# Feed-forward blocks with the tokens as stationary operand, gate and up in one 512-column product, the hidden product turned on TensorE, and the norm's root applied as a scale

## The chip, the cores and the metric

The kernel runs on one core of a Trainium2 chip. TensorE (PE) multiplies, VectorE (DVE) and ScalarE (ACT) do the elementwise work, GpSimd (POOL) a little of it, and the queue of SyncE (SP) issues the loads of the weights. The metric is the device time of one execution in microseconds (us); lower is better. Matrices are float32, at most 128 partitions high.

## The reference

The program is two layers of one block and one layer of a second block on 256 tokens of width 1024. Five feed-forwards of hidden width 2816 lie in it: two in each of the first two layers, one in the last. The change is about them and about nothing else.

```python
def rms_norm(x, gain):
    xf = x.astype(jnp.float32)
    y = xf * lax.rsqrt(jnp.mean(xf * xf, axis=-1, keepdims=True) + EPS)
    return (y * gain.astype(jnp.float32)).astype(x.dtype)

def swiglu_ffn(h, w_in, w_out):
    gate, up = jnp.split(h @ w_in, 2, axis=-1)
    return (jax.nn.silu(gate) * up) @ w_out

    for l in range(DEPTH):
        x = x + FFN_RESID * swiglu_ffn(rms_norm(x, ffn1_norm[l]), ffn1_w_in[l], ffn1_w_out[l])
...
        x = x + FFN_RESID * swiglu_ffn(rms_norm(x, ffn2_norm[l]), ffn2_w_in[l], ffn2_w_out[l])
...
        h = h + _swiglu(_rmsnorm(h, norm_ffn_g[l]), w_gate[l], w_up[l], w_down[l])
```

The root of the norm is one number per token. It can be taken out of a product: with g the gain and r the root's reciprocal, (x * r * g) @ w is r times (x * g) @ w.

## The kernel before

**Numbers in two halves.** A product of two float32 matrices is made of three products of a faster 32-bit form (`fp32r`): each operand is split into a rounded part `hi` and the rest `lo`, and TensorE adds hi by hi, hi by lo and lo by hi (`three`, L237 to 241). ACT makes `hi` by a copy (`split_act`, L453), DVE makes `lo` by a subtraction (`split_vec`, L459), for the weights as for the activations.

**Tokens.** The 256 tokens lie in two tiles of 128 (`m`). `x` holds them with tokens on the partitions. For a product they must lie with the width on the partitions: TensorE turns 128x128 squares into one of four banks `turn` (`norm_pe`, L367 to 375), DVE multiplies by the gain on the way to `xT` (L343), then ACT and DVE make `xT_hi` and `xT_lo` (L387, L392). `quarter b` is one half of the width of one tile.

**The feed-forward.** The hidden width is cut into 11 blocks of 256. A block takes two chunks of weights of 1 MB, one of gate and one of up, through a ring of four slots that SP fills (`ffn_sync`). In `block` (L465) the weights are the stationary operand, 128 columns at a time, and all 256 tokens move past them: four groups of 8 steps of three matmuls, 96 matmuls with 256 columns. Gate lands in one bank of `acc`, up in the other, hidden width on the partitions. ACT takes the silu of the gate bank (L554), DVE multiplies by the up bank (L584), and the product is already turned as the second product needs it: ACT copies `hT_hi` (L559), DVE makes `hT_lo` (L590). The split weights `w_hi` and `w_lo` have room for two blocks, so the split of block j+1 begins when block j-1 is done. After the 11 blocks, `down` (L506) multiplies by 11 chunks of `w_out`; there the tokens are the stationary operand and 512 columns of weights move. Its last four chunks are used for tile 0 first, so that tile 0 is ready four half steps before tile 1.

**The opening of a feed-forward** is the place between two products. DVE adds the product to `x` (L612), ACT takes the sum of squares (L310) and the root (L313), DVE its reciprocal (L337) and the scaled `xn` (L339), TensorE turns it, and the chain above follows. To have work in that time, TensorE does the first gate chunk without a split, in plain float32 and tile by tile (`first_gate`, L494); DVE and ACT split the first up chunk meanwhile.

**What sets the order.** Each engine runs a list written out by hand (`ffn_pe`, `ffn_act`, `ffn_vec`, `norm_act`, `add_norm_vec`), in order, and waits on counting semaphores. Nothing is scheduled by a tool: an instruction that waits holds back all behind it on its engine. `between` is the place in the last product of a stage at which TensorE turns tile 0 for the next one; `asides` are parameters of the next stage.

The openings are of three kinds: at the **start** of the program; after an output projection (**projection to feed-forward**, three times: both layers and the last); and from the second feed-forward of layer 0 straight into the first of layer 1 (**feed-forward to feed-forward**, once).

## Time and profile before

| | us |
|---|---|
| Median of 3 runs | 1775.39 (1773.43 to 1776.05) |
| The profiled execution | 1776.37 |
| Its span in the trace | 1774.7 |
| PE busy (share of the span) | 1747.2 (98%) |
| DVE busy | 1037.3 (58%) |
| ACT busy | 826.7 (47%) |

The profiled execution lies 0.98 us above the median of the runs, and 1.7 us of it lie outside the span. The granted TensorE clock was 0.997 of full speed on average. TensorE's matmuls overlap in the records (the next starts while the last drains), so the distance from start to start is what one costs.

### The profile page before, as it was taken

Reading aid. Unit: us, or ns where it says so; the run is one execution under the profiler, and the core shown is the slowest. Engines: PE = TensorE matmul, PEld = TensorE weight load, DVE = VectorE, ACT = ScalarE, POOL = GpSimd, SP = SyncE. Lnnn points to the kernel's source line nnn. Section 1 sums busy time; section 2 is a strip of 40 time slices with the busy share of each in tenths; the row PEclk is TensorE's granted clock in tenths of the full one; section 3 lists DMA queues with packets and bytes.
Section 4 is the critical chain, followed back from the end, with each engine's and each line's share of the span. In section 5 each row is a group of like instructions: output and inputs, shape, how many; then the busy total and the mean of one; then the engine's idle time right before and its main releaser. Section 6 shows DMA issues by size and latency. Waiting matters only on the chain.

```text
span 1774.7 us, 27727 instructions
## 1 busy us (share of the span) xinstructions
PE 1747.2 (98%) x11748; PEld 1545.3 (87%) x11748; DVE 1037.3 (58%) x1224; ACT 826.7 (47%) x913; POOL 71.0 (4%) x121
## 2 busy tenths in 40 slices
PE   8999999999999999999999999999999899999998
PEld 8998797887999899987978889998888766889996
DVE  5455466977655455454668785446688525644553
ACT  5544355563654445553555645455233114445442
POOL 0000000000000000000000000200191000000000
PEclk9999999999999999999999999999999999999999
DMA  7547254544655645372554446846347224356371
GB/s 261 189 137 281 83 182 156 159 149 143 221 176 185 225 153 179 120 281 89 186 164 144 145 143 233 161 160 236 121 158 138 65 80 144 118 170 205 100 286 58
DMA packets 202510, 292.13 MB, mean 165 GB/s; under 512 B 16834, under 2 KB 137908, under 8 KB 202420
## 3 DMA queue, kind: packets, MB, share of 16 engines
q1 hardware_dynamic: 201492, 290.21, 49.4%
q0 software_dynamic: 608, 0.60, 1.1%
q8 instruction: 70, 1.15, 0.3%
q14 instruction: 20, 0.16, 0.0%
q10 hardware_dynamic: 320, 0.01, 0.0%
HBM read 288.96 MB, written 1.84 MB: 164 GB/s over the span
## 4 chain that ended last, share of the span: by engine, by line
PE 92%; DVE 5%; DMA 2%; issue 1%; ACT 1%; ACTq 0%; DVEq 0%; SPq 0%
PE acc L239 24%; PE acc L240 23%; PE acc L241 23%; PE acc L286 3%; PE acc L2808 2%; DMA ring<-in_ffn_w_in 2%; PE acc L222 2%; PE acc L3118 1%; PE acc L494 1%; PE acc L207 1%; PE turn L2870 1%; PE acc L268 1%; PE turn L374 1%; PE acc L1353 1%; PE turn L1458 1%
## 5 line engine op out<-in xcount | busy, mean ns | idle before, releaser
L461 DVE TENSOR_TENSOR w_lo<-ring,w_hi 128x2048 fp32r<-128x2048 f32 x160 | 361.8, 2290 | 208.6 <-ACT w_hi L457 208.5
L239 PE MATMUL acc<-xT_hi,w_hi 128*128 128x256 f32 x1680 | 476.8, 284 | 2.9 <-DVE w_lo L461 2.1
L240 PE MATMUL acc<-xT_lo,w_hi 128*128 128x256 f32 x1680 | 476.2, 283 | 0.0
L241 PE MATMUL acc<-xT_hi,w_lo 128*128 128x256 f32 x1680 | 476.1, 283 | 0.0
L457 ACT ACTIVATE w_hi<-ring 128x2048 fp32r<-128x2048 f32 x160 | 300.8, 1911 | 142.9 <-PE acc L241 99.6
L239 PEld LDWEIGHTS acc<-xT_hi,w_hi 128*128 128x128 f32 x1680 | 322.6, 192 | 4.1 <-DVE w_lo L461 2.3
L241 PEld LDWEIGHTS acc<-xT_hi,w_lo 128*128 128x128 f32 x1680 | 322.7, 192 | 0.0
L240 PEld LDWEIGHTS acc<-xT_lo,w_hi 128*128 128x128 f32 x1680 | 322.6, 192 | 0.0
L239 PE MATMUL acc<-w_hi,hT_hi 128*128 128x512 f32 x440 | 172.6, 392 | 0.0
L241 PE MATMUL acc<-w_hi,hT_lo 128*128 128x512 f32 x440 | 171.3, 389 | 0.0
L240 PE MATMUL acc<-w_lo,hT_hi 128*128 128x512 f32 x440 | 171.3, 389 | 0.0
L554 ACT ACTIVATE big<-acc 128x512 f32<-128x512 f32 x55 | 32.9, 597 | 229.4 <-PE acc L241 229.4
L584 DVE TENSOR_TENSOR big<-big,acc 128x512 f32<-128x512 f32 x55 | 37.8, 687 | 152.9 <-ACT big L554 152.9
L240 PE MATMUL acc<-ring_lo,normed_hi 128*128 128x512 f32 (+2 forms) x288 | 108.4, 376 | 0.0
L239 PEld LDWEIGHTS acc<-w_hi,hT_hi 128*128 128x128 f32 x440 | 82.6, 188 | 18.9 <-ACT big L554 2.1
L241 PEld LDWEIGHTS acc<-w_hi,hT_lo 128*128 128x128 f32 x440 | 82.6, 188 | 17.2
L240 PEld LDWEIGHTS acc<-w_lo,hT_hi 128*128 128x128 f32 x440 | 82.7, 188 | 16.6
L310 ACT ACTIVATE xn<-x 128x1024 f32<-128x1024 f32 x20 | 21.2, 1058 | 130.2 <-DVE x L612 129.8
L235 DVE TENSOR_TENSOR ring_lo<-ring,part_hi 128x2048 fp32r<-128x2048 f32 x28 | 63.3, 2286 | 9.0 <-ACT part_hi L230 9.0
L612 DVE SCALAR_TENSOR_TENSOR x<-acc,x 128x512 f32<-128x512 f32 x36 | 24.0, 688 | 71.0 <-PE acc L241 71.0
L240 PEld LDWEIGHTS acc<-ring_lo,normed_hi 128*128 128x128 f32 x288 | 54.1, 188 | 9.3
L230 ACT ACTIVATE part_hi<-ring 128x2048 fp32r<-128x2048 f32 x28 | 52.8, 1915 | 14.7 <-DMA ring<-in_w_out 10.8
(543 smaller groups left out, 2878.5 us busy)
## 6 DMA issues: line engine op xcount, KB each, us to landing
ring<-in_ffn_w_in SPq DMA_DIRECT2D x88, 1024.0 KB, 6.0
ring<-in_w_in SPq DMA_DIRECT2D x52, 1024.0 KB, 5.1
ring<-in_ffn_w_out SPq DMA_DIRECT2D x44, 1024.0 KB, 6.2
ring<-in_w_branch SPq DMA_DIRECT2D x12, 1024.0 KB, 5.0
ring<-in_w_out SPq DMA_DIRECT2D x12, 1024.0 KB, 5.0
ring<-in_w_gate SPq DMA_DIRECT2D x11, 1024.0 KB, 5.1
ring<-in_w_up SPq DMA_DIRECT2D x11, 1024.0 KB, 6.3
ring<-in_w_down SPq DMA_DIRECT2D x11, 1024.0 KB, 5.4
```

What stands on the lines that cost most here:

```text
L222: ins = pe.matmul(acc[bank(G, m)][:, :], aT[:, 4 * i + k, m * P:(m + 1) * P], slot(c + i, 4, 512)[:, k, :], start=(i == 0 and k == 0), sto ...
L230: act.activation(hi[:, e % RING], slot(c, k, n), ACT.Copy).then_inc(s.hi, 1)
L235: vec.tensor_tensor(slot_lo(c, k, n), slot(c, k, n), hi[:, e % RING].bitcast(F32), ALU.subtract).then_inc(s.lo, 1)
L239: pe.matmul(o, a_hi, wh, start=start, stop=False)
L240: pe.matmul(o, a_hi, wl, start=False, stop=False)
L241: return pe.matmul(o, a_lo, wh, start=False, stop=stop)
L286: ins = pe.matmul(acc[bank(G, q)][:, (f % 2) * TOK:(f % 2) * TOK + TOK], w[:, k % kc, f * P:(f + 1) * P], aT[:, k, :], start=(k == 0), sto ...
L457: act.activation(w_part(w_hi, r), raw_part(c0, r), ACT.Copy).then_inc(f.hi, 1)
L461: vec.tensor_tensor(w_part(w_lo, r), raw_part(c0, r), w_part(w_hi, r).bitcast(F32), ALU.subtract).then_inc(f.lo, 1)
L554: act.activation(gate_s[:, jj % 2], acc[bank(G0 + jj, 0)][:, :].rearrange("p (k n) -> p k n", k=2), ACT.Silu).then_inc(acc_read[bank(G0 + ...
L584: vec.tensor_tensor(h_s[:, jj % 2], gate_s[:, jj % 2], acc[bank(G0 + jj, 1)][:, :].rearrange("p (k n) -> p k n", k=2), ALU.mult).then_inc( ...
L2808: ins = pe.matmul(acc[bank(G, m)][:, :], memT[:, 4 * i + k, m * P:(m + 1) * P], slot(c, 4, 512)[:, k, :], start=(i == 0 and k == 0), stop= ...
```

## The change

In all five feed-forwards:

- The tokens become the stationary operand. The two chunks of a block stand side by side as one moving operand of 512 columns, gate in 0 to 255 and up in 256 to 511. A block is 2 tiles by 8 steps by three matmuls, 48 matmuls with 512 columns, each tile in a bank of its own.
- The hidden product then has tokens on its partitions. TensorE turns it (`turn_hidden`), 4 squares of 128x128 for a block, between the two tiles of the next block; the last block's turn lies in the first step of `down`. `hT_hi` and `hT_lo` are made from the bank `turn`.
- The norm is folded (`Fold`, `fold_act`, `fold_vec`, `fold_turn_pe`): TensorE turns `x` itself; the root's reciprocal enters as the scale of the silu and as the scalar of DVE's multiplication (one `scalar_tensor_tensor`). `xn` is no longer made there, and nothing of the product waits for the root.
- The first gate chunk is split like all others and multiplied in `fp32r`. At the start of the program, where chunks land one after another, the first block is done in two halves of 256 columns.
- The release of split room goes by whole blocks (`r | 1`). For the third and fifth feed-forward the two halves of the split room are swapped (`swap`), so that the first chunks can be split while the last product still runs.
- The last four chunks of `down` are used for tile 1 in the order 8, 9, 7, 10 (before: 7, 8, 9, 10), and in the second feed-forward `between` comes one step earlier.

The norms ahead of the mixers, the mixers, the cross attention and the final norm are as before.

```diff
-            def first_gate():
-                if not turned:
-                    norm_pe(pe, n, tiles=(0,))
-                wait_chunk(pe, c0)
-                wait_acc_free(pe, G0, 0)
-                for m in range(MT):
-                    if m == 1:
-                        norm_pe(pe, n, tiles=(1,))
-                    for ft in range(2):
...
+            def first_block():
+                wh, wl = w_pair(f, w_hi, 0), w_pair(f, w_lo, 0)
+                for c, width, chunks in ((0, FB, 1), (FB, FB, 2)) if n.first else ((0, 2 * FB, 2),):
+                    cs = slice(c, c + width)
+                    for m in range(MT):
+                        o, ms = acc[bank(G0, m)][:, cs], slice(m * P, (m + 1) * P)
+                        if m == 0:
+                            pe.wait_ge(f.hi, f.w0 + chunks)
+                        if c == 0:
+                            pe.wait_ge(n.act, n.hi(2 * m + 1))
+                            wait_acc_free(pe, G0, m)
                         for k in range(KD):
-                            if ft == 0 and k % 4 == 0:
-                                pe.wait_ge(n.vec, n.turned(2 * m + k // 4))
-                            ins = pe.matmul(acc[bank(G0, 0)][:, ft * TOK + m * P:ft * TOK + (m + 1) * P],
-                                            raw_part(c0, 0)[:, k, ft * P:(ft + 1) * P], xT[:, k, m * P:(m + 1) * P],
-                                            start=(k == 0), stop=(k == KD - 1))
-                ins.then_inc(products_done, 1)
-            first_gate()
-            pe.wait_ge(n.vec, n.v0 + SPLIT_DONE)
-            block(0, halves=(1,))
-            block(1)
-            with pe.Fori(1, PAIRS) as i:
-                block(0, i)
+                            pe.matmul(o, xT_hi[:, k, ms], wh[:, k, cs], start=(k == 0), stop=False)
+                        if c == 0:
+                            pe.wait_ge(n.vec, n.lo(2 * m + 1))
+                        for k in range(KD):
+                            if c == 0 and m == 0 and k == 4:
+                                fold_turn_pe(pe, n, 1)
+                            pe.matmul(o, xT_lo[:, k, ms], wh[:, k, cs], start=False, stop=False)
+                        if m == 0:
+                            pe.wait_ge(f.lo, f.w0 + RING + chunks)
+                        for k in range(KD):
+                            ins = pe.matmul(o, xT_hi[:, k, ms], wl[:, k, cs], start=False, stop=(k == KD - 1))
+                        if chunks == 2 and m == 0:
+                            ins.then_inc(f.tile, 1)
+                ins.then_inc(products_done, 2)
...
+            def turn_hidden(jj, i=0):
+                for m in range(MT):
+                    wait_acc_read(pe, G0 + jj, m, i)
+                pe.wait_ge(f.hT_lo, f.h0 + jj + 1 + 2 * i)
+                for ft in range(2):
+                    for m in range(MT):
+                        ins = pe.transpose(turn[2 + jj % 2][:, ft * TOK + m * P:ft * TOK + (m + 1) * P],
+                                           h_s[:, jj % 2, m, ft * P:(ft + 1) * P], ident[:, :])
+                ins.then_inc(f.turned, 1)
+            def block(jj, i=0):
+                pe.wait_ge(f.lo, f.w0 + RING + 2 * jj + 2 + RING * i)
+                products(jj, 0, i).then_inc(f.tile, 1)
+                turn_hidden(jj - 1, i)
+                products(jj, 1, i).then_inc(products_done, 2)
...
+        def fold_act(act, n, f, c0):
+            def root(m):
+                n.there(act, m)
+                act.activation(xn[:, m, :], x[:, m, :], ACT.Square, accum_out=stat[:, m:m + 1]).then_inc(n.act, 1)
+                act.wait_ge(n.act, n.rooted(m) - 1)
+                act.activation(stat[:, 2 + m:3 + m], stat[:, m:m + 1], ACT.Sqrt, bias=eps_col[:, 0:1],
+                               scale=1.0 / D).then_inc(n.act, 1)
+            def halves(m):
+                for b in range(2 * m, 2 * m + 2):
+                    act.wait_ge(n.vec, n.turned(b))
+                    act.activation(quarter(xT_hi, b), quarter(xT, b), ACT.Copy).then_inc(n.act, 1)
+            root_there_act(act)
+            if not n.first:
+                split_act(act, f, c0, 0)
+                split_act(act, f, c0, 1)
+            root(0)
+            halves(0)
+            split_act(act, f, c0, 0 if n.first else 2)
+            halves(1)
+            root(1)
+            if n.first:
+                split_act(act, f, c0, 1)
+                split_act(act, f, c0, 2)
+            split_act(act, f, c0, 3)
...
+        def fold_vec(vec, n, f, c0, gain, add=None, weights_first=False):
...
+            if add:
+                add(vec, 0, 0)
+                if weights_first:
+                    add(vec, 1, 0)
+                    split_vec(vec, f, c0, 0)
+                add(vec, 0, 1)
+                if weights_first:
+                    split_vec(vec, f, c0, 1)
+            turned(0)
+            turned(1)
+            rest(0)
+            rest(1)
+            scale(0)
+            if not weights_first:
+                split_vec(vec, f, c0, 0)
+            if add:
+                if not weights_first:
+                    add(vec, 1, 0)
+                add(vec, 1, 1)
+            if not weights_first and not n.first:
+                split_vec(vec, f, c0, 1)
+            turned(2)
+            turned(3)
+            rest(2)
+            rest(3)
+            if n.first:
+                split_vec(vec, f, c0, 1)
+                scale(1)
+                split_vec(vec, f, c0, 2)
+            else:
+                split_vec(vec, f, c0, 2)
+                scale(1)
+            split_vec(vec, f, c0, 3)
...
+            for j, i in enumerate((KF // 2 - 3, KF // 2 - 2, KF // 2 - 4, KF // 2 - 1)):
+                if between and j == (2 if f.q == 1 else 3):
                     between(pe)
...
-            def silu(jj, i=0):
-                wait_products(act, c0 + 2 * jj + 1, i)
-                act.activation(gate_s[:, jj % 2], acc[bank(G0 + jj, 0)][:, :].rearrange("p (k n) -> p k n", k=2),
-                               ACT.Silu).then_inc(acc_read[bank(G0 + jj, 0)], 1)
+        def ffn_act(act, f, n, c0, G0, asides={}):
+            def silu(jj, m, i=0):
+                if m == 0:
+                    act.wait_ge(f.tile, f.h0 + jj + 1 + 2 * i)
+                else:
+                    wait_products(act, c0 + 2 * jj + 1, i)
+                act.activation(gate_s[:, jj % 2, m, :], acc[bank(G0 + jj, m)][:, 0:FB], ACT.Silu,
+                               scale=stat[:, 4 + m:5 + m]).then_inc(f.gate, 1)
...
-            def hidden(jj, i=0):
-                wait_acc_read(vec, G0 + jj, 0, i)
-                vec.tensor_tensor(h_s[:, jj % 2], gate_s[:, jj % 2], acc[bank(G0 + jj, 1)][:, :].rearrange(
-                    "p (k n) -> p k n", k=2), ALU.mult).then_inc(acc_read[bank(G0 + jj, 1)], 1)
+            def hidden(jj, m, i=0):
+                vec.wait_ge(f.gate, 2 * f.h0 + 2 * jj + m + 1 + 4 * i)
+                vec.scalar_tensor_tensor(out=h_s[:, jj % 2, m, :], in0=acc[bank(G0 + jj, m)][:, FB:2 * FB], scalar=stat[:, 4 + m:5 + m],
+                                         in1=gate_s[:, jj % 2, m, :], op0=ALU.mult,
+                                         op1=ALU.mult).then_inc(acc_read[bank(G0 + jj, m)], 1)
```

In the lists below `chunk_landed` is the ring's semaphore, `x` at an `acc_read` wait means both adds of a tile, and `x2` counts equal instructions in a row.

DVE, the opening from a projection to a feed-forward (layer 0), before:

```order
L612 SCALAR_TENSOR_TENSOR x<-acc,x 128x512 [waits tile0_done] x2
L337 RECIPROCAL stat<-stat 128x1 [waits norm_act_steps]
L339 TENSOR_SCALAR xn<-x,stat 128x1024 [waits norm_vec_steps]
L612 SCALAR_TENSOR_TENSOR x<-acc,x 128x512 [waits products_done]
L343 TENSOR_TENSOR xT<-turn,col 128x4x128 [waits norm_pe_steps] x2
L612 SCALAR_TENSOR_TENSOR x<-acc,x 128x512 [waits products_done]
L392 TENSOR_TENSOR xT_lo<-xT,xT_hi 128x4x128 [waits norm_act_steps] x2
L337 RECIPROCAL stat<-stat 128x1 [waits norm_act_steps]
L339 TENSOR_SCALAR xn<-x,stat 128x1024 [waits norm_vec_steps]
L343 TENSOR_TENSOR xT<-turn,col 128x4x128 [waits norm_pe_steps] x2
L461 TENSOR_TENSOR w_lo<-ring,w_hi 128x8x256 [waits w_hi_ready]
L392 TENSOR_TENSOR xT_lo<-xT,xT_hi 128x4x128 [waits norm_act_steps] x2
```

and now:

```order
L748 SCALAR_TENSOR_TENSOR x<-acc,x 128x512 [waits tile0_done]
L748 SCALAR_TENSOR_TENSOR x<-acc,x 128x512 [waits products_done]
L492 TENSOR_TENSOR w_lo<-ring,w_hi 128x8x256 [waits w_hi_ready]
L748 SCALAR_TENSOR_TENSOR x<-acc,x 128x512 [waits tile0_done]
L492 TENSOR_TENSOR w_lo<-ring,w_hi 128x8x256 [waits w_hi_ready]
L532 TENSOR_TENSOR xT<-turn,col 128x4x128 [waits norm_pe_steps] x2
L538 TENSOR_TENSOR xT_lo<-xT,xT_hi 128x4x128 [waits norm_act_steps] x2
L543 RECIPROCAL stat<-stat 128x1 [waits norm_act_steps]
L748 SCALAR_TENSOR_TENSOR x<-acc,x 128x512 [waits products_done]
L532 TENSOR_TENSOR xT<-turn,col 128x4x128 [waits norm_pe_steps] x2
L538 TENSOR_TENSOR xT_lo<-xT,xT_hi 128x4x128 [waits norm_act_steps] x2
L492 TENSOR_TENSOR w_lo<-ring,w_hi 128x8x256 [waits w_hi_ready]
```

The first two splits of weights (L492) have moved ahead of the second add of tile 0 and ahead of the work on the turned tile.

ACT at the same opening, before:

```order
L298 ACT_TABLE_LOAD
L298 ACTIVATE stat<-eps_col 128x1
L310 ACTIVATE xn,stat<-x 128x1024 [waits acc_read2,acc_read0]
L313 ACTIVATE stat<-stat,eps_col 128x1 [waits norm_act_steps]
L457 ACTIVATE w_hi<-ring 128x8x256 [waits products_done,chunk_landed1]
L387 ACTIVATE xT_hi<-xT 128x4x128 [waits norm_vec_steps] x2
L310 ACTIVATE xn,stat<-x 128x1024 [waits acc_read3,acc_read1]
L313 ACTIVATE stat<-stat,eps_col 128x1 [waits norm_act_steps]
L387 ACTIVATE xT_hi<-xT 128x4x128 [waits norm_vec_steps] x2
```

and now:

```order
L324 ACT_TABLE_LOAD
L324 ACTIVATE stat<-eps_col 128x1
L488 ACTIVATE w_hi<-ring 128x8x256 [waits products_done,chunk_landed0]
L488 ACTIVATE w_hi<-ring 128x8x256 [waits products_done,chunk_landed1]
L506 ACTIVATE xn,stat<-x 128x1024 [waits acc_read2,acc_read0]
L508 ACTIVATE stat<-stat,eps_col 128x1 [waits norm_act_steps]
L514 ACTIVATE xT_hi<-xT 128x4x128 [waits norm_vec_steps] x2
L488 ACTIVATE w_hi<-ring 128x8x256 [waits products_done,chunk_landed2]
L514 ACTIVATE xT_hi<-xT 128x4x128 [waits norm_vec_steps] x2
L506 ACTIVATE xn,stat<-x 128x1024 [waits acc_read3,acc_read1]
L508 ACTIVATE stat<-stat,eps_col 128x1 [waits norm_act_steps]
L488 ACTIVATE w_hi<-ring 128x8x256 [waits products_done,chunk_landed3]
```

Both splits of the first two chunks (L488) stand ahead of the squares of tile 0, and no table is loaded between them and the last split.

PE, the first block at the same place, now (before it were 16 plain matmuls, a turn of tile 1, 16 more, and 48 of 256 columns):

```order
L267 MATMUL acc<-part_hi,xT_rest 128x512
L592 MATMUL acc<-w_hi,xT_hi 128x512 x8
L598 MATMUL acc<-w_hi,xT_lo 128x512 x4
L500 MATMUL turn<-ident,x 128x128 x8
L598 MATMUL acc<-w_hi,xT_lo 128x512 x4
L602 MATMUL acc<-w_lo,xT_hi 128x512 x8
L592 MATMUL acc<-w_hi,xT_hi 128x512 x8
L598 MATMUL acc<-w_hi,xT_lo 128x512 x8
```

The turn of tile 1 (L500) stands in the middle of tile 0's second group and is fed by `x`, no longer by `xn`.

## Rows read from the trace of the kernel before

**Rows 1.** The page, busy time and instructions of each engine.

```profile
PE 1747.2 (98%) x11748; PEld 1545.3 (87%) x11748; DVE 1037.3 (58%) x1224; ACT 826.7 (47%) x913; POOL 71.0 (4%) x121
```

**Rows 2.** Groups by line and form: busy us, mean ns | idle before, releaser.

```profile
L239 PE MATMUL acc<-xT_hi,w_hi 128*128 128x256 f32 x1680 | 476.8, 284 | 2.9 <-DVE w_lo L461 2.1 <-DVE xT_lo L392 0.8
...
L461 DVE TENSOR_TENSOR w_lo<-ring,w_hi 128x2048 fp32r<-128x2048 f32 x160 | 361.8, 2290 | 208.6 <-ACT w_hi L457 208.5
...
L457 ACT ACTIVATE w_hi<-ring 128x2048 fp32r<-128x2048 f32 x160 | 300.8, 1911 | 142.9 <-PE acc L241 99.6 <-DMA ring<-in_ffn_w_in 32.5 <-DMA ring<-in_ffn_w_out 5.0
...
L240 PEld LDWEIGHTS acc<-w_lo,hT_hi 128*128 128x128 f32 x440 | 82.7, 188 | 16.6
```

**Rows 3.** Timeline of PE in a steady gate and up block: start us, us, instruction.

```profile
60.04 0.28 PE L239 MATMUL acc<-xT_hi,w_hi 128*128 128x256 f32 x1
...
63.64 0.28 PE L239 MATMUL acc<-xT_hi,w_hi 128*128 128x256 f32 x1
```

**Rows 4.** Timeline of PE in the second product, 512 columns.

```profile
160.36 0.39 PE L239 MATMUL acc<-w_hi,hT_hi 128*128 128x512 f32 x1
...
162.40 0.39 PE L239 MATMUL acc<-w_hi,hT_hi 128*128 128x512 f32 x1
```

**Rows 5.** Timeline of PE, five squares turned between matmuls (layer parameters).

```profile
178.72 0.23 PE L998 MATMUL turn<-ident,vecs 77*128 77x77 f32 x1
178.79 0.60 PE L1000 MATMUL turn<-ident,ws_in 128*128 128x128 f32 x4
179.15 0.47 PE L239 MATMUL acc<-w_hi,hT_hi 128*128 128x512 f32 x1
179.46 0.39 PE L240 MATMUL acc<-w_lo,hT_hi 128*128 128x512 f32 x1
```

**Rows 6.** Timeline of PE, eight squares turned between matmuls (tile 0 of a norm).

```profile
635.83 1.03 PE L374 MATMUL turn<-ident,xn 128*128 128x128 f32 x8
...
636.62 0.47 PE L239 MATMUL acc<-w_hi,hT_hi 128*128 128x512 f32 x1
...
636.94 0.39 PE L240 MATMUL acc<-w_lo,hT_hi 128*128 128x512 f32 x1
```

**Rows 7.** Timeline of ACT, silu of the first block at the start.

```profile
25.32 0.60 ACT L554 ACTIVATE big<-acc 128x512 f32<-128x512 f32 x1 [2.50 <-PE acc L241]
```

**Rows 8.** Timeline, opening after a projection: first adds (DVE), first silu (ACT).

```profile
442.20 1.29 DVE L612 SCALAR_TENSOR_TENSOR x<-acc,x 128x512 f32<-128x512 f32 x2 [5.99 <-PE acc L241]
...
463.41 0.60 ACT L554 ACTIVATE big<-acc 128x512 f32<-128x512 f32 x1 [2.50 <-PE acc L241]
```

**Rows 9.** The same two rows of the opening between two feed-forwards.

```profile
627.87 1.29 DVE L612 SCALAR_TENSOR_TENSOR x<-acc,x 128x512 f32<-128x512 f32 x2 [6.57 <-PE acc L241]
...
654.47 0.60 ACT L554 ACTIVATE big<-acc 128x512 f32<-128x512 f32 x1 [2.50 <-PE acc L241]
```

**Rows 10.** Timeline at the start: PE's turn, ACT's copies and a root.

```profile
8.30 1.73 PE L374 MATMUL turn<-ident,xn 128*128 128x128 f32 x8
...
10.12 1.31 ACT L387 ACTIVATE xT_hi<-xT 128x512 fp32r<-128x512 f32 x2 [4.31 <-DVE xT L343]
11.34 1.04 ACT L310 ACTIVATE xn<-x 128x1024 f32<-128x1024 f32 x1
...
12.50 0.29 ACT L313 ACTIVATE stat<-stat,eps_col 128x1 f32<-128x1 f32 x1
```

**Rows 11.** Timeline of PE, two long waits in the last layer's mixer.

```profile
1379.19 2.46 PE L2745 MATMUL turn<-ident,big 128*128 128x128 f32 x16 [1.75 <-DVE big L2718]
...
1394.54 1.09 PE L2790 MATMUL turn<-ident,big 128*128 128x128 f32 x8 [3.56 <-DVE big L2783]
```

**Rows 12.** Stretches around these waits: busy us of engines, PEclk, DMA share, GB/s.

```profile
1375.00:1385.00 10.00, 7.54 (x124) 6.15 (x113) 9.56 (x19) 0.31 (x1) 0.00 (x0) 1.00 0.01 2
...
1395.00:1405.00 10.00, 9.89 (x96) 8.00 (x94) 2.50 (x7) 3.39 (x8) 0.00 (x0) 0.83 0.00 0
```

**Rows 13.** DMA view of 440 to 480 us, GB/s in each of 40 us.

```profile
GB/s 374 37 0 0 0 0 169 388 369 161 250 365 347 24 25 17 0 0 27 265 389 360 374 387 386 385 387 348 382 386 378 377 361 373 387 312 37 6 0 0
```

## What the change will do to the time

> **What bounds the kernel now.** The busy shares come first: TensorE works in 98% of the span [rows 1]. That says where the limit is, not how hard TensorE works, so the groups by line come second. In the gate and up products of one feed-forward, L239 to 241, TensorE runs three groups of 1680 matmuls, DVE's subtractions wait for ACT's copies and ACT's copies for TensorE [rows 2]; TensorE itself waited 2.9 us in 477 there. Third is the distance from start to start in the timeline, the price of one matmul. With 256 columns, 30 matmuls take 63.64 - 60.04 = 3.60 us, 0.1200 each [rows 3]; a block of 96 takes 11.52. With 512 columns and the tokens stationary, 9 take 2.04, 0.2267 each [rows 4]. So only what TensorE is given to do, and what it waits for at the openings, can change the time.
>
> **Steady blocks: the matmuls.** 48 matmuls of 512 columns replace 96 of 256: 48 x 0.2267 = 10.88 us against 11.52, a gain of 0.64 a block. The row for 512 columns has the same roles (tokens stationary, weights moving) and the same number form, so I take it as it is. Ten blocks of each of five feed-forwards are of this kind: 50 x 0.64 = 32.0 us gained.
>
> **Steady blocks: the turns.** Each block now has 4 squares turned. Where 5 squares stood between matmuls, one of them 77 wide, the first matmul should have started at 178.72 and the second at 178.94; the second started at 179.46, 0.52 later [rows 5]. Without the narrow square (some 0.07) four cost 0.45. Eight squares put the second matmul from 636.05 to 636.94, 0.89 later, 0.11 each [rows 6]: four by half of it are 0.44, and 0.49 if the delay of the first matmul behind them (0.32 instead of 0.23) is paid in full each time. I take 0.45, nearest to the case of four. Blocks 1 to 10: 50 x 0.45 = 22.5 us; the turn of the last block in the second product: 5 x 0.45 = 2.25. The steady part is 32.0 - 22.5 - 2.25 = 7.25 us gained, between 5 (0.49) and 7.8 (0.44).
>
> **What hides the rest of a block.** The silu and the product of one tile are half as long as before and twice as many. After the end of a block ACT does a silu (some 0.4), then two copies of 1.9 us, DVE the subtractions of 2.25 behind them [rows 2]: 0.4 + 1.9 + 2 x 2.25 + 0.2 = 7.0 us, needed after 11.33. The turn in the middle of a block needs the last silu and product, ready 1.2 us after the block's start and reached after 5.44. ACT's table loads leave the loop; nobody waited for them, so they bring nothing. SP's list loses one wait, and its loads keep their order; each takes some 4.5 us where two are wanted every 11.3: two chunks alone in the queue moved from 446 to 449.4 and from 450 to 453.1 [rows 13], and their slots came free, by the list of the code, 2.7 us after tile 0 of the projection (444.7) and at its end (448.4).
>
> **The three openings after a projection.** Time runs from the first add of tile 0. Before: first silu at 463.41 - 442.20 = 21.2, block 1 starts 0.2 earlier, 21.0 [rows 8]. Now, with adds and multiplications of tiles at 0.65 and the prices above: TensorE reaches the turn of tile 0 at 2.5. DVE does two adds (1.3), the subtraction that has moved ahead (3.5), and only then the second add of tile 0 (4.2): TensorE waits 1.8 us. The turn ends at 5.25, the projection at 7.95. DVE, behind a second subtraction until 6.4, has the turned quarters at 7.7, ACT the rounded ones at 8.4: TensorE waits 0.55 and starts block 0 at 8.5. The groups of 8 and 4 end at 11.2, the turn of tile 1 at 12.1, tile 0 at 14.85, tile 1 (ready at 14.6) at 20.3. The last two subtractions end at 19.3, in time. Block 1 starts at 20.3 instead of 21.0: 0.7 gained, three times 2.1. The norm has left the path; what is late next is DVE with its subtractions. With no wait at all it would be 3.0 each (see the second case).
>
> **The opening between two feed-forwards.** Before: 654.47 - 627.87 = 26.6, block 1 at 26.4 [rows 9]. Now ACT may split the first two chunks only when half of the last four chunks is used (5.4), and has them before squares and root (10.7) and before the rounded tile 0 (12.0). TensorE ends the product at 11.6, waits 0.5, is held at the turn of tile 1 until 16.6 because DVE has a subtraction ahead of the two adds of tile 1 (1.7), then for the second subtraction (0.4). Block 1 starts at 26.4. Nothing gained, nothing lost.
>
> **The start.** Before, the plain float32 gate product began as soon as tile 0 was turned and multiplied, and block 1 began at 25.1 [rows 7]. TensorE turns tile 0 at 8.30, the rounded tile is there at 11.43, and ACT then does squares and root (until 12.8 for tile 1 before) [rows 10]. Now the first matmul needs a split chunk, which ACT copies behind these copies, 11.4 to 13.3. TensorE, idle since 10.0, starts at 13.4. Its first half groups lead to the turn of tile 1 at 15.9; DVE and ACT have tile 1 at 17.7, the root ends at 19.1, ACT splits the second chunk until 21.0, and three subtractions follow: block 1 at 28.1, 3.0 later than before. That is at full clock. After a wait of 3.56 us the stretch behind it ran at a mean clock of 0.83 [rows 11, 12], which is 1.7 us of work lost in 10; after one of 1.75 it stayed at 1.00. A wait of 3.4 is nearest to the first, and the part that falls on the chain is 1.4: I take +4.4, with +3.0 as the other end.
>
> **The sum.** -7.25 - 2.1 + 0 + 4.4 = -4.95, say -5.0. Against the profiled execution, 1776.37: 1771.4. The median of the runs is 0.98 lower, 1775.39, so I forecast **1770.4**. A measurement of this kernel can tell about 0.2%, 3.6 us, from no change.
>
> **Rivals.** Each is worked out on top of the forecast.
> (a) The openings do not wait, because DVE and ACT are further ahead than I count: 11.8 us for block 0 with its turn instead of 14.8, 3.0 less at each. That is 3 x 2.3 + 3.0 + 7.4 = 17.3 more, 1753; half of it is 1762. For it: the weights are there early. Against it: the order of DVE's list, which puts 2.2 us ahead of an add for which TensorE is idle.
> (b) The clock falls at the four later openings too, 1.7 each: +6.8, 1777.2, no change. For it: waits of 1.8 and 1.7 us are new there. Against it: the stretch with the 1.75 us wait.
> (c) Slower. A turn stands behind three semaphores, which the loop counts through registers. If TensorE cannot load the next stationary operand ahead of such a wait, each turn pays a weight load of 0.19 [rows 2]: 55 x 0.19 = 10.5, 1780.9. It decides the sign from 0.09 a turn on. For it: none of the turns in the trace stands in a loop. Against it: 192 matmuls of two looped blocks take their 23.04 us with such waits among them, and the eight squares of rows 6 stand behind a wait.
> (d) Slower by far: long matmuls do not save a fixed part here. By rows 3 and 4 the fixed part is 2 x 0.1200 - 0.2267 = 0.0133 us. Were it 0.0025, the gain of 50 blocks would be 6 us instead of 32, and the time 1796. The row with 512 columns is the very form that is to run, which leaves this little room.
>
> The Trainium skill, "TensorE: Matmul & The Clock Gate", section "Wait — 56ns, not 53.3ns?", gives a fixed cost of about 2.5 ns for a warm matmul, which is case (d) and speaks against the change. This case's trace disagrees: 13.3 ns a matmul in both sizes. By the page the time would be near 1796.
>
> **How the numbers follow.** Forecast 0.60 (of it 0.50 gains over 0.2%, 0.10 less); (a) 0.12; (b) 0.14, no change; (c) 0.12; (d) 0.02. Faster 0.62, same 0.24, slower 0.14. For eight in ten the range leaves out (d), most of (c) and the far half of (a), and takes in the turn's price (2 us), the start (1.4) and (b): 1764.5 to 1777.5.
>
> **What would show it.** In the trace after: a steady block from silu to silu of 11.33 us (11.52 before); 0.227 between matmuls; four turned squares that put the second matmul behind them 0.45 off. From the first add to block 1, 20.3 after a projection, 26.4 between feed-forwards; block 1 of the program at 28 to 29.5. TensorE idle 1.8 at the turn of tile 0 after a projection, with DVE's subtraction ahead of the add. The prediction is wrong at its root if a block is not near 11.33, and in its size if the openings differ by over 1 us each.

## The result and the profile after

The changed kernel takes **1781.52 us** (median of 16 runs, 1777.15 to 1784.06), the kernel before 1775.07 (16 runs, 1773.43 to 1780.25). The ratio is 1.0031, 95% interval 1.0023 to 1.0039: **slower by 0.3%**, where 0.3% faster was forecast (1770.4 us, range 1764.5 to 1777.5), and outside the range. The profiled execution took 1783.62 us, 2.1 above its median, with a span of 1781.9 (before 1774.7).

The page of the changed kernel, busy time and instructions, answers to [rows 1]: 2452 matmuls fewer and 11 us less work on TensorE, and a longer span.

```profile
PE 1736.3 (97%) x9296; PEld 1426.1 (80%) x9296; DVE 1048.3 (59%) x1274; ACT 794.2 (45%) x928; POOL 70.9 (4%) x121
```

The groups by line and form answer to [rows 2]. What to see is the last column: the first matmul of a block, L265, stood idle for 11.9 us behind DVE's subtraction of the weights, where L239 before had 2.9 in all.

```profile
L265 PE MATMUL acc<-w_hi,xT_hi 128*128 128x512 f32 x800 | 317.9, 397 | 11.9 <-DVE w_lo L492 11.9
...
L265 PE MATMUL acc<-w_hi,hT_hi 128*128 128x512 f32 x440 | 172.5, 392 | 0.7 <-DVE big L712 0.7
```

A steady block, in the timeline of TensorE: from the turn of one block to that of the next are 80.66 - 69.31 = 11.35 us, and the second matmul behind the four turned squares starts at 69.98, 0.67 after the first of them, where a spacing of 0.2267 alone gives 0.23.

```profile
69.31 0.60 PE L622 MATMUL turn<-ident,big 128*128 128x128 f32 x4
69.66 0.48 PE L265 MATMUL acc<-w_hi,xT_hi 128*128 128x512 f32 x1
69.98 0.39 PE L266 MATMUL acc<-w_lo,xT_hi 128*128 128x512 f32 x1
...
80.66 0.60 PE L622 MATMUL turn<-ident,big 128*128 128x128 f32 x4
```

Here are the idle stretches of TensorE in the gate and up blocks, from the same timeline (in brackets the idle time and what ended it). 29.68 is block 1 of the program. 1146.67 is a block in the middle of the last feed-forward of the second layer. The other five are all block 10, the last of its feed-forward.

```profile
29.68 0.49 PE L265 MATMUL acc<-w_hi,xT_hi 128*128 128x512 f32 x1 [0.46 <-DVE w_lo L492]
...
132.94 0.50 PE L265 MATMUL acc<-w_hi,xT_hi 128*128 128x512 f32 x1 [0.80 <-DVE w_lo L492]
...
570.72 0.50 PE L265 MATMUL acc<-w_hi,xT_hi 128*128 128x512 f32 x1 [0.82 <-DVE w_lo L492]
...
761.22 0.50 PE L265 MATMUL acc<-w_hi,xT_hi 128*128 128x512 f32 x1 [1.29 <-DVE w_lo L492]
...
1146.67 0.79 PE L265 MATMUL acc<-w_hi,xT_hi 128*128 128x512 f32 x1 [6.51 <-DVE w_lo L492]
...
1206.81 0.50 PE L265 MATMUL acc<-w_hi,xT_hi 128*128 128x512 f32 x1 [0.96 <-DVE w_lo L492]
...
1703.07 0.50 PE L265 MATMUL acc<-w_hi,xT_hi 128*128 128x512 f32 x1 [1.08 <-DVE w_lo L492]
```

**Why block 10.** The timelines of SP, ACT and DVE follow the last pair of chunks of the first feed-forward. SP asks for both at 120.82, which is when the products of block 8 end; the first is there at 125.97, the second at 128.65; DVE is through with it at 132.89.

```profile
120.82 1.00 SPq L464 DMA_DIRECT2D ring<-in_ffn_w_in  x2
```

```profile
125.97 1.92 ACT L488 ACTIVATE w_hi<-ring 128x2048 fp32r<-128x2048 f32 x1 [4.67 <-DMA ring<-in_ffn_w_in]
128.65 1.92 ACT L488 ACTIVATE w_hi<-ring 128x2048 fp32r<-128x2048 f32 x1 [0.75 <-DMA ring<-in_ffn_w_in]
```

```profile
127.93 2.29 DVE L492 TENSOR_TENSOR w_lo<-ring,w_hi 128x2048 fp32r<-128x2048 f32 x1 [6.10 <-ACT w_hi L488]
130.60 2.29 DVE L492 TENSOR_TENSOR w_lo<-ring,w_hi 128x2048 fp32r<-128x2048 f32 x1 [0.38 <-ACT w_hi L488]
```

The chunks inside the loop are asked for as soon as their slot is free. Those of block 9 were asked for at 91.56 and 93.74, 29 and 27 us ahead of that block's start at 120.63:

```profile
91.56 0.37 SPq L464 DMA_DIRECT2D ring<-in_ffn_w_in  x1
93.74 0.37 SPq L464 DMA_DIRECT2D ring<-in_ffn_w_in  x1
```

The last two stand behind the loop, where SP also waits for the products of block 8, a wait that nothing needs (both kernels have it). They are asked for only 11.3 us ahead of the time at which block 10 could have begun (132.94 - 0.80). In the kernel before they came just as late, and it did not matter, because a block took its gate chunk at its start and its up chunk 5.8 us later. A matmul of 512 columns takes gate and up at once. **The change moved the deadline of every second chunk half a block forward.** Before, in DVE's timeline, the up chunk of block 10 was ready at 127.23 + 2.29 = 129.52, in a block that started at 128.80 (DVE, then TensorE).

```profile
127.23 2.29 DVE L461 TENSOR_TENSOR w_lo<-ring,w_hi 128x2048 fp32r<-128x2048 f32 x1 [0.23 <-ACT w_hi L457]
```

```profile
128.80 0.28 PE L239 MATMUL acc<-xT_hi,w_hi 128*128 128x256 f32 x1
```

The block at 1146 is the same deadline met by another delay. In both kernels an up chunk is held up until 1142, while GpSimd's small parameter loads hold the queues. Before, TensorE was by then in the middle of the block and waited 2.1 us [rows 2]; now it had not begun and waited 6.5. The row of before:

```profile
1146.13 0.42 PE L239 MATMUL acc<-xT_hi,w_hi 128*128 128x256 f32 x1 [2.10 <-DVE w_lo L461]
```

Behind the idle time the granted clock is at its lower level (1.2 of 2.4 GHz) for most of six us, 0.56 in the mean, where the kernel before had 0.72 over the same six. In the two stretches the columns are busy us of PE, PEld, DVE, ACT and POOL, the clock, the DMA share and GB/s.

```profile
1110.00:1140.00 30.00, 30.00 (x139) 24.65 (x137) 12.68 (x11) 8.75 (x10) 8.71 (x14) 1.00 0.85 92
...
1146.00:1152.00 6.00, 5.33 (x14) 4.29 (x15) 6.00 (x6) 3.15 (x2) 1.16 (x1) 0.56 0.90 301
```

### The profile page after: what moved, and what is told of

It reads as the page before. It is cut to its first block, busy times and chain, and to the rows that moved or that the text cites. A ratio compares the mean times of both kernels' runs of the same rounds, so it can differ in the third digit from the quotient of the medians.

```text
span 1781.9 us, 22954 instructions
## 1 busy us (share of the span) xinstructions
PE 1736.3 (97%) x9296; PEld 1426.1 (80%) x9296; DVE 1048.3 (59%) x1274; ACT 794.2 (45%) x928; POOL 70.9 (4%) x121
## 4 chain that ended last, share of the span: by engine, by line
PE 87%; DVE 6%; DMA 5%; ACT 2%; issue 1%; SPq 0%; ACTq 0%; DVEq 0%
PE acc L265 21%; PE acc L266 21%; PE acc L267 21%; DMA ring<-in_ffn_w_in 3%; PE acc L312 3%; DVE w_lo L492 2%; PE acc L2949 2%; PE acc L248 2%; ACT w_hi L488 1%; PE turn L622 1%; PE acc L3259 1%; PE acc L233 1%; PE turn L3011 1%; PE acc L592 1%; PE acc L602 1%; PE acc L294 1%
## 5 line engine op out<-in xcount | busy, mean ns | idle before, releaser
L492 DVE TENSOR_TENSOR w_lo<-ring,w_hi 128x2048 fp32r<-128x2048 f32 x165 | 374.0, 2289 | 201.2 <-ACT w_hi L488 200.9
L488 ACT ACTIVATE w_hi<-ring 128x2048 fp32r<-128x2048 f32 x165 | 311.1, 1913 | 187.4 <-PE acc L267 124.3
L265 PE MATMUL acc<-w_hi,xT_hi 128*128 128x512 f32 x800 | 317.9, 397 | 11.9 <-DVE w_lo L492 11.9
L267 PE MATMUL acc<-w_hi,xT_lo 128*128 128x512 f32 x800 | 312.8, 391 | 0.0
L266 PE MATMUL acc<-w_lo,xT_hi 128*128 128x512 f32 x800 | 312.5, 391 | 0.0
L265 PEld LDWEIGHTS acc<-w_hi,xT_hi 128*128 128x128 f32 x800 | 150.9, 189 | 44.5 <-issue 7.9
L677 ACT ACTIVATE big<-acc,stat 128x256 f32<-128x256 f32 x110 | 52.0, 473 | 280.3 <-PE acc L267 273.4
L267 PEld LDWEIGHTS acc<-w_hi,xT_lo 128*128 128x128 f32 x800 | 150.7, 188 | 32.0
L266 PEld LDWEIGHTS acc<-w_lo,xT_hi 128*128 128x128 f32 x800 | 151.0, 189 | 29.8
L265 PE MATMUL acc<-w_hi,hT_hi 128*128 128x512 f32 x440 | 172.5, 392 | 0.7 <-DVE big L712 0.7
L712 DVE SCALAR_TENSOR_TENSOR big<-acc,stat,big 128x256 f32<-128x256 f32 x110 | 52.7, 480 | 183.4 <-ACT big L677 183.4
L265 PEld LDWEIGHTS acc<-w_hi,hT_hi 128*128 128x128 f32 x440 | 82.6, 188 | 18.0 <-DVE big L712 1.1
L1082 DVE TENSOR_TENSOR ring_lo<-ring,early_hi 128x2048 fp32r<-128x2048 f32 (+2 forms) x24 | 49.0, 2042 | 13.8 <-ACT early_hi L1072 13.7
```

Of the source, the lines that this page charges most:

```text
L265: pe.matmul(o, a_hi, wh, start=start, stop=False)
L266: pe.matmul(o, a_hi, wl, start=False, stop=False)
L267: return pe.matmul(o, a_lo, wh, start=False, stop=stop)
L488: act.activation(w_part(f, w_hi, r), raw_part(c0, r), ACT.Copy).then_inc(f.hi, 1)
L492: vec.tensor_tensor(w_part(f, w_lo, r), raw_part(c0, r), w_part(f, w_hi, r).bitcast(F32), ALU.subtract).then_inc(f.lo, 1)
L677: act.activation(gate_s[:, jj % 2, m, :], acc[bank(G0 + jj, m)][:, 0:FB], ACT.Silu, scale=stat[:, 4 + m:5 + m]).then_inc(f.gate, 1)
```

## The experiments

Three theories are told apart. "A" is the theory of the deadline, "B" that the new order of ACT's and DVE's lists makes the waits, "C" that the loads have become slower. The times are medians of 4 to 12 runs. Differences are to the changed kernel's 1781.52 us unless said otherwise, and each ratio is to the kernel before, run beside it (1774.29 to 1775.33).

**1. The last pair asked for early.**

```diff
-                elif r < N_IN:
+                elif r < RING:
                     sync.wait_ge(products_done, c0 + r + 1)
```

> The changed kernel with one wait taken from SP: the load of a gate or up chunk whose place in the sequence is past the first four no longer waits for a product, only for its slot (as the loads in the loop do). Theory A (the second chunk's deadline): a block of 512 columns needs both chunks when it starts, where before it needed the up chunk half a block later; the last pair of each feed-forward is asked for only at the end of block 8 and comes too late for block 10. Then the five waits of block 10 (0.80 + 0.83 + 1.29 + 0.96 + 1.08 = 4.96 us) go, and perhaps the 0.65 in front of the first product of the output, while the wait of 6.5 us in the last feed-forward of the second layer stays: 5.0 to 5.6 us less than the changed kernel, about 1776, a ratio to the kernel before of 1.000 to 1.001. Theory B (the queues' order): ACT's and DVE's lists now place silus and copies behind the splits that wait for a load, and the wait would only move to the next load, the output weights, which are no earlier: at most 1 us less, about 1781. Theory C (the loads themselves are slower in the changed kernel): the waits shrink by a part, 1 to 3 us less.

Measured: 1773.57 us, ratio to before 0.9992 (0.9983 to 1.0001), 8.0 less than the changed kernel. The timeline of SP shows the last four loads asked for by 105.79, and block 10 has no idle time in front of it in any of the five feed-forwards, nor has the first output product.

```profile
91.96 13.79 SPq L464 DMA_DIRECT2D ring<-in_ffn_w_in  x4
105.79 0.54 SPq L1026 DMA_DIRECT2D vecs<-in_mix_norm  x1
```

Theory A. B is out: the lists are untouched, and the wait did not move to the next load. The gain is 2.4 us over the 5.6 expected. Between the two profiled executions it is 9.9, and 2.2 of that is that the long wait, said to stay at 6.5, was 4.29 here. It was 4.6 to 5.3 in experiments 5, 8 and 9, which leave its cause in place, so the profiled execution that gave 6.5 seems to be at the high end. How much of the 2.4 between the medians is this wait is not shown.

**2. The same edit in the kernel before.**

> The kernel before with the same wait taken from SP as in the early-pair run. Theory A: there the last pair's gate chunk was in time and the up chunk was needed 5.8 us later, so nothing waited: no change, within 0.5 us of the kernel before. If the kernel before too lost time at these late loads (theory C), it would be 1 to 5 us faster.

Measured: 1776.02 us, ratio 1.0002 (0.9994 to 1.0011): no change, as A says. The late loads were there and cost nothing.

**3. Nothing but the deadline, in the kernel before.**

```diff
-                        pe.wait_ge(f.lo, f.w0 + RING + 2 * jj + 1 + half + RING * i)
+                        pe.wait_ge(f.lo, f.w0 + RING + 2 * jj + 2 + RING * i)
```

> The kernel before with nothing changed but the deadline: a block waits for the subtractions of both its chunks at its start, where it waited for the up chunk's only in front of its up half. Its matmuls, its orders and its loads are those of the kernel before. Theory A: in the rows of before the up chunk of block 10 is ready 0.7, 0.7, 1.0, 0.9 and 1.1 us after the block's start (129.52 against 128.80, and so on), 4.4 us in all, and the one behind the small loads 7.9 us after the block's start where 2.1 were waited for: 5.8 more. Together 10 us more than the kernel before, 11 with a clock that falls in the longer wait: a ratio of 1.006. Theory B (it is the order of ACT's and DVE's lists in the changed kernel that makes the waits): this kernel has the old lists, so 1 us at most. Theory C (the loads are slower in the changed kernel): none, 0 to 1 us.

Measured: 1788.19 us, ratio 1.0074 (1.0060 to 1.0088), 12.9 more than the kernel before beside it (1775.33), where 10 to 11 were expected. In the view of waits, and two of the six in the timeline:

```profile
PE acc L239 <- DVE w_lo L461: 12.2, 6, 8.3
```

```profile
129.58 0.39 PE L239 MATMUL acc<-xT_hi,w_hi 128*128 128x256 f32 x1 [0.49 <-DVE w_lo L461]
...
1149.66 0.58 PE L239 MATMUL acc<-xT_hi,w_hi 128*128 128x256 f32 x1 [8.31 <-DVE w_lo L461]
```

This settles it. With old matmuls, old lists and old loads, the deadline alone brings the six waits: 12.2 us where 2.1 were, 10.1 more, as expected. B and C are not needed for them. What makes the last 2 us of the 12.9 is open.

**4. Chunks cut by depth.** A chunk holds gate and up together for half of the contraction, so the second is due 2.7 us later than in the changed kernel. Each chunk now comes as two transfers of half the size, and the program's first block goes by half depths too, so the edit changes more than the deadline.

```diff
-                return w_pair(f, w, r // 2)[:, :, (r % 2) * FB:(r % 2 + 1) * FB]
+                return w_pair(f, w, r // 2)[:, (r % 2) * 4:(r % 2 + 1) * 4, :]
...
                 for k in range(KD):
+                    if m == 0 and k == 4:
+                        pe.wait_ge(f.lo, f.w0 + RING + 2 * jj + 2 + RING * i)
...
-                pe.wait_ge(f.lo, f.w0 + RING + 2 * jj + 2 + RING * i)
+                pe.wait_ge(f.lo, f.w0 + RING + 2 * jj + 1 + RING * i)
...
```

> The changed kernel with its chunks cut the other way: a chunk is gate and up together for half of the contraction (k 0 to 3, then k 4 to 7), each loaded as two transfers of half the size, so that a block needs its second chunk only in the middle of its first tile, 2.7 us after its start. The first block of the program goes by half depths of 512 columns instead of gate and up of 256. Theory A: the five waits of block 10 (4.96 us) go, the 6.5 us become 3.8, and the start gains 0.5 to 1 us: 8 to 9 us less than the changed kernel, about 1773, faster than the kernel before by 0.1%. Theory B: the waits stand behind ACT's order, which is the same, so at most 1 us less. Theory C: twice as many transfers make the loads no faster, at most 2 us less.

Measured: 1768.42 us, ratio 0.9960 (0.9948 to 0.9972), 13.1 less than the changed kernel, 4 to 5 more than expected. No wait at block 10, and 0.73 us where the long one was:

```profile
1138.90 0.50 PE L266 MATMUL acc<-w_hi,xT_hi 128*128 128x512 f32 x1 [0.73 <-DVE w_lo L503]
```

The wait fell by 5.8 and not by 2.7. The other 3 us are that the chunk was there earlier in the course of its block: ACT takes it at 1134.60, 0.7 us before the block could start, and in the changed kernel at 1142.30, 2.3 us behind it. Whether the cut did this or chance is not shown. The clock did not fall there either: behind the wait of 6.5 TensorE had worked for 4.6 us at half rate, which costs 2.3 us, and those were not in the expectation. The start gained 0.9: the turn of its first hidden block stands at 34.35, was 35.24. The first output product of the first feed-forward still waits 0.77 us.

**5. The small loads spread.** GpSimd's small loads were set apart over eight blocks; the two of the log_dt stayed where they were.

> The changed kernel with GpSimd's parameter loads of the second layer's last feed-forward spread over eight blocks, where 13 of 15 were asked for in a row at one block. Everything else is as it was. Theory A says that these small loads hold up the ring's chunk at 1113 to 1142 us in both kernels, and that the earlier deadline turned a wait of 2.1 us into one of 6.5: the wait of 6.5 us should fall to under 2, 4.5 to 6.5 us less than the changed kernel, about 1776; the five waits of block 10 stay. If the chunk is late for another reason (theory B: ACT reached its copy late; theory C: slower loads in general), the wait stays near 6.5 and the time within 1 us of the changed kernel.

Measured: 1781.11 us, ratio 1.0030 (1.0020 to 1.0040): no gain, and the wait is 4.6 us, within what it is in kernels that leave these loads alone. The expectation failed, and the trace says why. With the others out of the way the DMA share (the last but one column) is high while almost nothing arrives (2 GB/s), and the view of DMA issues (KB each, median us to landing) leaves one suspect: two loads of 64 x 16 single elements take 20 us each, and those that in the changed kernel stood behind them and took 21 to 24 take 3 to 6.

```profile
1115.00:1118.00 3.00, 3.00 (x15) 2.50 (x14) 0.48 (x1) 1.55 (x2) 0.00 (x0) 1.00 1.97 2
```

```profile
wsT<-in_s_log_dt POOLq DMA_DIRECT2D x2, 4.0 KB, 20.1
vecs<-in_conv_w POOLq DMA_DIRECT2D x1, 24.0 KB, 2.9
```

**6. The log_dt as one load of whole rows**, from which GpSimd copies every second element.

```diff
-            for g in range(2):
-                pool.dma_start(s5w[64 * g:64 * g + 64, 0, :],
-                               t["s5_log_dt_2"].rearrange("o (k g) -> g (o k)", g=2)[g:g + 1, :].broadcast_to([64, NS]),
...
+            pool.dma_start(ldt[:, :], t["s5_log_dt_2"].broadcast_to([P, 2 * NS])).then_inc(ldt_in, 16)
...
+            for g in range(2):
+                pool.tensor_copy(s5w[64 * g:64 * g + 64, 0, :],
+                                 ldt[64 * g:64 * g + 64, :].rearrange("p (k g) -> p k g", g=2)[:, :, g]).then_inc(ldt_copied, 1)
```

> The changed kernel, but the two small loads of s5_log_dt, each of 64 x 16 single elements, are one load of contiguous rows of 32 into a buffer of its own, from which GpSimd copies every second element. The run with the spread loads still had the small loads of the log_dt where they were and still lost 4.6 us at the block that starts at 1143. Theory A (these two loads, 20 us from issue to landing, hold up the ring's chunk, and the block needs that chunk at its start): the wait of 4.3 to 6.5 us goes, and with it the half clock behind it, 5 to 8 us less than the changed kernel, 1774 to 1776.5. Theory B (all the small loads together, or the ring's chunk alone): less than 1.5 us gained.

Measured: 1774.05 us, ratio 0.9996 (0.9987 to 1.0005), 7.5 less. No block in the middle of that feed-forward waits for its weights any more. The load lands after 6.5 us, and in the same 30 us 217 GB/s arrive where 92 did:

```profile
ldt<-in_s_log_dt POOLq DMA_DIRECT2D x1, 16.0 KB, 6.5
```

```profile
1110.00:1140.00 30.00, 30.00 (x140) 24.92 (x139) 14.88 (x14) 12.67 (x14) 7.36 (x15) 1.00 0.69 217
```

The view of DMA has the queue of GpSimd's loads by itself: packets, MB, share of the time of the 16 DMA engines, from 1110 to 1140 us, in the changed kernel and then in this run.

```profile
q0 software_dynamic: 379, 0.13, 57.6%
```

```profile
q0 software_dynamic: 432, 0.21, 5.7%
```

So it was these two loads: without them the queue moves more in a tenth of the engines' time. In experiment 5, where they stand there almost alone, it takes 57.4% for 0.02 MB. The Trainium skill, "DMA: Bandwidth & Descriptors", section "Why small descriptors are slow (HBM only)", names a fixed cost for each small piece that a transfer is made of; the two runs agree in direction, at 16 KB in 6.5 us against 4 KB in 20 (17.6 in the changed kernel). No run shows that this cost alone makes the 20 us.

**7. The same edit in the kernel before.**

> The kernel before with the log_dt loaded as one load of contiguous rows. The small loads cost it a wait of 1.8 to 2.1 us and some 1.5 us of half clock behind it: 2 to 3.5 us less than the kernel before, a ratio of 0.998 to 0.999. It tells how much of what the all-together kernel gains is open to the kernel before as well.

Measured: 1772.28 us, ratio 0.9983 (0.9974 to 0.9992), 3.05 less than the kernel before: the 2.1 us of wait and some clock. The same two loads cost the changed kernel more than twice as much.

**8. The start: the first copies early.**

```diff
             root(0)
+            if n.first:
+                split_act(act, f, c0, 0)
             halves(0)
-            split_act(act, f, c0, 0 if n.first else 2)
+            split_act(act, f, c0, 1 if n.first else 2)
             halves(1)
             root(1)
             if n.first:
-                split_act(act, f, c0, 1)
                 split_act(act, f, c0, 2)
```

Two copies move: that of the first chunk goes ahead of the rounded tile 0, and that of the second chunk from behind the root of tile 1 into its place.

> The changed kernel with ACT's list at the program's start in another order: the copy of the first chunk stands ahead of the two copies of the turned x (ACT idles 4.5 us there), and that of the second chunk directly behind them. The question is what the start's 4.6 us are made of. Theory A (ACT's order): TensorE waited 3.25 us at 14.05 for the first copy; it then begins 1.9 us earlier, the last subtraction of DVE before block 1 ends 1.9 to 2.5 us earlier, and block 1 starts at 27.2 to 27.8 where it started at 29.68: 2 us less than the changed kernel, 1779.5. Theory B (the work itself: the products moved behind the splits, the clock at half rate from 14 to 18 us): the order matters little, 0 to 0.5 us less. If the shorter wait also keeps the clock up, up to 2 us more are gained: 1777.5.

Measured: 1775.71 us, ratio 1.0007 (0.9998 to 1.0016), 5.8 less. The first product starts at 12.13 (14.05 in the changed kernel) and the clock stays at full (2.4 GHz) in this run; from 14 to 18 us it had been granted at 0.57. The turn in block 1 stands at 31.15, was 35.24: 4.1 us of the start's 4.6 came from where two copies stood in ACT's list, some 1.7 of them by way of the clock (an estimate: 43% of the four us at 0.57). The expectation had 1777.5 at best, with the clock's part. ACT took the first chunk as soon as it was there:

```profile
8.97 1.92 ACT L488 ACTIVATE w_hi<-ring 128x2048 fp32r<-128x2048 f32 x1 [2.16 <-DMA ring<-in_ffn_w_in]
```

```profile
12.13 0.59 PE L593 MATMUL acc<-w_hi,xT_hi 128*128 128x256 f32 x3 [1.73 <-issue]
...
31.15 0.60 PE L623 MATMUL turn<-ident,big 128*128 128x128 f32 x4
```

**9. The openings behind a projection: the second add early.**

```diff
                 add(vec, 0, 0)
-                if weights_first:
-                    add(vec, 1, 0)
-                    split_vec(vec, f, c0, 0)
                 add(vec, 0, 1)
                 if weights_first:
-                    split_vec(vec, f, c0, 1)
+                    split_vec(vec, f, c0, 0)
...
             if add:
-                if not weights_first:
-                    add(vec, 1, 0)
+                add(vec, 1, 0)
                 add(vec, 1, 1)
-            if not weights_first and not n.first:
+            if not n.first:
                 split_vec(vec, f, c0, 1)
```

> The changed kernel with DVE's list at the three openings behind a projection in another order: the second add of tile 0 directly behind the first, and the first subtraction of the weights behind both; the two adds of tile 1 ahead of the second subtraction. TensorE waited 1.49 us at each of these openings for the second add before it could turn x. Theory A (this wait is on the path that sets the end): 3 x 1.3 to 1.5 = 4 to 4.5 us less than the changed kernel, 1777. Theory B (DVE's list is full there, from 447.40 to 466.7 with 3 us of gaps, so that what is moved back is late in its turn): the wait comes back at the second tile's turn or at block 1, 0 to 1.5 us less, 1780 to 1781.5.

Measured: 1775.23 us, ratio 1.0003 (0.9994 to 1.0012), 6.3 less, where 4 to 4.5 were expected. Block 1 starts 464.93 - 446.90 = 18.0 us behind the first add, where the changed kernel had 20.1: 2.1 at each of three openings. Of it 1.7 are at the turn of tile 0 and the rest at block 0, whose rounded tile is there earlier. Theory A, and DVE's list was not full.

```profile
464.93 0.39 PE L265 MATMUL acc<-w_hi,xT_hi 128*128 128x512 f32 x1
```

**10. All of it.** The cut by depth with 6, 8 and 9; then the four small edits (1, 6, 8, 9) without the cut; then everything, with SP's parameter loads behind the first two output chunks.

> All that has an explanation together: the chunks cut by depth (that run: 1768.4, no wait at block 10), the first copies early, the second add early, and the log_dt in one row. If each works as its own run expects under theory A: 1768.4 - 2 - 4.3 - 1 = 1761, a ratio to the kernel before of 0.992. If the openings are bound by DVE's full list: 1765 to 1766.

> The changed kernel with the four edits that leave its chunks as they are: the last pair's loads early, the first copies early, the second add early, the log_dt in one row. Measured alone against the changed kernel they were worth 8.0, 5.8, 6.3 and 7.5 us by the medians (profiled executions also hold a clock that falls or not in the mixers). If the effects add up by their waits (5.6 + 4.1 + 4.5 + 6.5 + 1 to 2 of clock): 1781.5 - 22 = 1759.5, the same as the all-together kernel (1759.0), and the cut by depth is then not needed. If the cut by depth has a worth of its own beyond the waits: 1761 to 1763.

> The all-together kernel with the last pair's loads early too, and SP's sixteen parameter loads behind the first two output chunks and not ahead of them. The all-together kernel still waited 0.59 and 0.85 us for the product of block 10 in front of the output products, because ACT's list has a silu behind the copies of those two chunks. Theory A: both waits go, 1.0 to 1.4 us less: 1757.7. If the parameters come too late for their first user instead: 1759 to 1761.

Measured: 1759.00 us, ratio 0.9909 (0.9895 to 0.9922); 1756.20, ratio 0.9893 (0.9878 to 0.9908); 1756.33, ratio 0.9891 (0.9876 to 0.9906). All three are below what was expected, by 2.0, 3.3 and 1.4 us. The best is thus the change with the four small edits, **19 us or 1.1% under the kernel before** beside it (1775.33). Of these 19, the 3.05 of experiment 7 are open to the kernel before as well; against that kernel the gain is 16.1. The third kernel, with the cut and the parameter loads moved on top, is no faster than the second, so the cut by depth shows no worth of its own once the loads are in time. The page of the kernel with the four edits: its matmuls are those of the changed kernel, and the waits are gone.

```profile
span 1754.4 us, 22946 instructions
...
PE 1727.7 (98%) x9296; PEld 1422.6 (81%) x9296; DVE 1047.2 (60%) x1274; ACT 794.1 (45%) x928; POOL 70.5 (4%) x122
```

Against the changed kernel the four edits gain 25.3 us: more than their sum by waits (22), less than the sum of the four runs (27.6), which may each hold a part of the same clock's falls.

## Why the prediction was wrong

**Steady blocks: right.** 11.35 us a block where 11.33 was said; a turn puts the second matmul 0.67 - 0.23 = 0.44 off (0.45 said) and makes a block 11.35 - 10.88 = 0.47 longer; 0.2267 between matmuls. Case (c), a turn that pays a weight load behind a semaphore, did not come, though its 1780.9 us lie nearest to the result: the right size from the wrong mechanism. Case (d) did not come either. The Trainium skill, "TensorE: Matmul & The Clock Gate", section "Wait — 56ns, not 53.3ns?", would have had it, and this trace disagrees as the row for 512 columns did: 0.2267 us from start to start in the new blocks is 13.3 ns above 512 columns at 2.4 GHz, where the Trainium skill has about 2.5.

**Openings: right within a microsecond.** Behind a projection the turn waits 1.5 us (1.8 said) for DVE's second add, and block 1 starts at 467.54 - 447.40 = 20.1 (20.3 said); between the feed-forwards 25.6 (26.4 said).

```profile
451.64 1.06 PE L500 MATMUL turn<-ident,x 128*128 128x128 f32 x8 [1.50 <-DVE x L748]
...
467.54 0.39 PE L265 MATMUL acc<-w_hi,xT_hi 128*128 128x512 f32 x1
```

Case (a) was dismissed with the right argument, DVE's order, and experiment 9 shows how little stood in its way.

**The start: right in its sum.** Block 1 at 29.68, 4.6 us later than before, where 4.4 was said; the clock fell, as the larger of the two ends had it. Some luck is in it: 0.6 of the 4.6 is that the turn of tile 0 itself came at 8.89 where it was 8.30 before, which the prediction did not have.

**The step that failed is "What hides the rest of a block".** It worked out that the two chunks of a block are ready 7.0 us after a block's start and "needed after 11.33", from a block in the middle of the loop, and took it for all fifty. Two things were not asked. First, when does each chunk become due? The step knew that the new operand takes both at once, but counted only when they are made. Second, does every block get its chunks as the middle one does? Block 10 is loaded by lines behind SP's loop, with a wait of its own, and its chunks are asked for 11.3 us ahead of it where those of block 9 are asked for 29 and 27 us ahead. "Its loads keep their order" was true and beside the point: SP's wait cost nothing as long as the up chunk had half a block of grace. The one sign in the rows of before was the 2.1 us behind `w_lo` in [rows 2]. It marks a chunk that was already late for the later deadline, so it had to grow by up to 5.8 when the deadline moved; it was read as small and left alone.

The table goes by the profiled executions, 1776.37 before and 1783.62 after. Their difference of 7.25 is 12.2 above the -4.95 of the sum. Between the medians the miss is 11.1; the long wait of the profiled execution seems to be longer than usual (experiment 1). Of the 12.2:

| Term not in the sum | us |
|---|---|
| block 10, five times (0.80, 0.82, 1.29, 0.96, 1.08) | 4.95 |
| first output product behind block 10 | 0.65 |
| the long wait, 6.51 for 2.10 | 4.4 |
| half clock behind it (2.3 of work for 1.7) | 0.6 |
| steady blocks, 50 x 0.02 | 1.0 |
| start, 4.6 for 4.4 | 0.2 |
| last mixer, 302.1 for 301.2 from TensorE's turn ahead of it to the first add behind it | 0.9 |
| openings, better than said: 3 x 0.2 + 0.8 | -1.4 |
| found | 11.3 |

One microsecond stays unplaced. The mixer's 0.9 is the clock: in the ten us behind the same wait of 3.6 us its mean was 0.73, where the kernel before had 0.83. It varied from kernel to kernel (in experiment 6 it did not fall there at all), so it may be chance and not the change.

Of case (b), a clock that falls at the openings, nothing was seen: behind waits of 1.5 us it stayed at full.

## What to carry to other kernels

When two operands are merged into one, write down for each when it is due before and after, not only when it is ready. Then check the first and the last turn of a loop by their own code, since a load that is late and harmless becomes late and costly without a change in itself. A small wait that is already in the profile is one place where such a deadline will be missed. It is not the only one: at block 10 the kernel before had shown no wait at all, and there only the list of due times finds it.

## What the runs showed of the hardware

Two transfers of 4 KB in single elements, 17.6 to 20 us each, stood beside large loads that brought 92 GB/s over 30 us in the changed kernel, and 217 without them (experiment 6). GpSimd's queue took 57.6% of the DMA engines' time for 0.13 MB, and 5.7% without them.

The clock makes waits dearer than they are long. After 6.5 us idle TensorE worked 4.6 us at half rate; after 3.25 us at the start the clock fell too (0.57 from 14 to 18 us), after 1.73 us (experiment 8) not at all. The length of the wait alone does not decide it: after 2.1 us in the kernel before, the clock was 0.54 from 1147 to 1150 us, and after 3.55 us in the mixer of experiment 6 it stayed at 1.00. So a first product that started 1.9 us sooner, with the second chunk's copy early too, was worth 4.1.
